# A three-part block on one core: grouped attention turned by block transposes and transfers instead of TensorE, and an end in two halves

## The chip, the cores and the metric

The kernel runs on one core of a Trainium2 chip. The metric is the device time of one execution in microseconds; three executions of the kernel before gave 3020.45, 3019.07 and 3018.32 us, median 3019.07 us. A difference of about 0.2% (6 us) is what such runs can tell from no change.

## The reference

256 tokens of width 2048 pass through two layers and a third, larger block, all in float32. In short:

```python
# layers 0 and 1: u = rms_norm(x) @ w_in; layer 0 pools over 2, 4, 8 and 16 tokens, layer 1 has
# differential attention; both add cross attention to a memory, then x += [..] @ w_out,
# then x += relu(rms_norm(x) @ w_ff1)**2 @ w_ff2
xn = rms_norm_2(x, norm_pre_w); z = xn @ w_in_2            # 2048 -> 13312
u_lru, g_lru, q, k, v, g_attn, m_lru, m_attn = split(z)
h = rg_lru(conv(u_lru), forward) + rg_lru(conv(u_lru), backward)
y_a = h * silu(g_lru)
# 16 query heads in 4 groups over 4 key and value heads of 128, window of +-128 tokens
m = max(scores.max(-1), sink); e = exp(scores - m)
p = e / (e.sum(-1) + exp(sink - m))
y_b = einsum(p, v) * silu(g_attn)
merged = sigmoid(m_lru) * (y_a @ w_proj_a) + sigmoid(m_attn) * (y_b @ w_proj_b)
x = x + rms_norm_2(merged @ w_out_2, norm_post_w)
```

## The kernel before, in words

All matrix products stream weights. A product of 256 tokens with 512 columns of weights is a group; there are 128. A group is eight slabs of 256 weight rows. SyncE loads a slab (512 KB) into one of four buffers `raw`; ScalarE rounds it to `whi` (line 933), VectorE takes the rest `wlo` (line 1260), and TensorE multiplies: 12 products of 128x512 (lines 1790 to 1792), high by high, low by high and high by low, for two row tiles and two token tiles, into `acc0` or `acc1`. A slab's buffer is free once TensorE is through with it, so ScalarE and VectorE can be three slabs ahead.

Everything else hangs between slabs. `plan()` writes, for each engine, which step follows which slab; the engines run their lists in order and meet by semaphores. `attention(j, p)` places one attention job over two heads: `att_in` (TensorE turns queries, and for the grouped jobs keys, by products with the identity, lines 1839 and 1842) after slab p, `att_score` after p+1, `att_smx` and `att_exp` with p+4, `att_prob` with p+5, `att_pt` (eight turns of the probabilities, line 1859) after p+5, `att_pv` (line 1871) after p+6, `att_ot` (four turns of the output, line 1931) after p+7, and `att_o`, `att_hi`, `att_lo` behind. Four jobs are memory attention (two in each layer, placed by `attention` or `roomy`), eight are the grouped attention of the third block. These eight follow one another, one per group of eight slabs. VectorE runs up to three slabs ahead of TensorE, and its step of slab s stands behind its `wlo` of slab s. The softmax scales the output, not the probabilities, by the inverse sum (`att_o`, line 1561), and then by the gate, which GpSimd loads back from DRAM (`gate_load`, line 859).

Where the kernel turns a whole group's output (`turned`), it does so without TensorE: VectorE transposes 32x32 blocks (`turn`, line 1385), and GpSimd moves the blocks to their partitions by 16 transfers of 32 KB (`shuffle`, line 899). One output is still turned on TensorE among the gate groups (`tail`, line 1808). `pool_mix` (lines 1949 to 1951) multiplies each of 12 tiles by the parts of a band matrix that aren't zero.

At the end, `epi_last` squares and scales the last group (lines 1006, 1711), VectorE forms the mean square of both token tiles (`rms`, lines 1271 to 1278), scales and adds in four pieces (line 1766), and SyncE stores four pieces of 512 KB.

## Time and profile before

| | |
|---|---|
| median of three executions | 3019.07 us |
| the profiled execution, its span | 3018.06 us, 3016.3 us |
| PE, DVE, ACT, POOL busy | 2971.2, 1820.8, 1524.8, 442.6 us |
| granted clock over the span | 0.998 |
| share of 16 DMA engines, weight queue and GpSimd's queue | 57.5% and 5.8% |
| a transfer with 256 runs of 512 bytes (`lru_w`) on POOL | 0.72 us |
| a transfer of a shuffle on POOL | 0.50 us |

PE is TensorE, DVE VectorE, ACT ScalarE, POOL GpSimd, SP SyncE. A product is shown with its whole passage through the array (0.39 us for 512 columns), but starts one every 0.23 us, so times of blocks are read from start to start. An f32 product of the attention is recorded as two instructions. "Granted clock" is the share of 2.4 GHz that TensorE was given. An idle time in brackets is that of the engine before the row, with what ended it.

### The profile page before, as it was taken

How to read it: one execution, taken by the hardware profiler on the slowest of the kernel's cores; microseconds unless marked ns; L12 is line 12 of the kernel's file. 1: busy time of each engine (PE TensorE's matmuls, PEld its weight loads, DVE VectorE, ACT ScalarE, POOL GpSimd, SP SyncE). 2: the span in 40 equal slices, each digit the busy share in tenths (PEclk: the TensorE clock that was granted, in tenths of full speed). 3: DMA queues.
4: the chain of work that ended last, by engine and by line, in shares of the span. 5: the costliest groups of instructions: out<-in, count | busy, mean ns of one | idle time of the engine just before them, and what ended most of it. 6: DMA issues, size and time to landing. Idle time of an engine off the chain costs nothing.

```text
span 3016.3 us, 37365 instructions
## 1 busy us (share of the span) xinstructions
PE 2971.2 (99%) x13524; PEld 2461.1 (82%) x13524; DVE 1820.8 (60%) x2399; ACT 1524.8 (51%) x2036; POOL 442.6 (15%) x881
## 2 busy tenths in 40 slices
PE   8999999999999999999999999999999999999998
PEld 7888888888888778778888888888888888787886
DVE  6437555555555776866545555556546668786554
ACT  6535444444444665755434444445445557785443
POOL 0003302011023310012203020122000233010210
PEclk9999999999999999999999999999999999999999
DMA  7556766666567655556666666677666566665774
GB/s 261 168 158 204 217 195 201 204 191 214 180 216 231 205 172 168 152 180 199 216 189 214 192 198 207 188 224 230 199 195 191 175 190 192 192 204 200 248 247 153
DMA packets 326765, 600.08 MB, mean 199 GB/s; under 512 B 31440, under 2 KB 56400, under 8 KB 325840
## 3 DMA queue, kind: packets, MB, share of 16 engines
q1 hardware_dynamic: 293248, 541.13, 57.5%
q0 software_dynamic: 32784, 55.89, 5.8%
q8 instruction: 101, 1.65, 0.2%
q10 hardware_dynamic: 576, 0.94, 0.1%
q14 instruction: 56, 0.46, 0.0%
HBM read 561.15 MB, written 10.49 MB: 190 GB/s over the span
## 4 chain that ended last, share of the span: by engine, by line
PE 89%; DVE 5%; ACT 4%; issue 1%; DMA 0%; DVEq 0%; ACTq 0%; SPq 0%
PE acc L1790 28%; PE acc L1792 28%; PE acc L1791 28%; ACT whi L933 1%; DVE wlo L1255 1%; DVE wlo L1260 1%; PE sd L1871 1%; PE sd L1853 1%; PE tp L1808 1%; ACT prob L1170 1%; PE tp L1960 1%; ACT qk L1178 0%; PE sd L1974 0%; ACT whi L936 0%; PE sd L1859 0%
## 5 line engine op out<-in xcount | busy, mean ns | idle before, releaser
L1790 PE MATMUL acc<-whi,set_hi 128*128 128x512 f32 x4096 | 1616.0, 395 | 16.6 <-DVE wlo L1260 11.0
L1792 PE MATMUL acc<-whi,set_lo 128*128 128x512 f32 x4096 | 1598.2, 390 | 0.0
L1791 PE MATMUL acc<-wlo,set_hi 128*128 128x512 f32 x4096 | 1597.2, 390 | 0.0
L1260 DVE TENSOR_TENSOR wlo<-raw,whi 128x1024 fp32r<-128x1024 f32 x944 | 1136.2, 1221 | 712.9 <-ACT whi L933 711.8
L933 ACT ACTIVATE whi<-raw 128x1024 fp32r<-128x1024 f32 x944 | 980.2, 1057 | 844.8 <-PE acc L1792 672.5
L1790 PEld LDWEIGHTS acc<-whi,set_hi 128*128 128x128 f32 x4096 | 770.5, 188 | 187.2 <-DVE wlo L1260 17.1
L1792 PEld LDWEIGHTS acc<-whi,set_lo 128*128 128x128 f32 x4096 | 769.9, 188 | 161.5
L1791 PEld LDWEIGHTS acc<-wlo,set_hi 128*128 128x128 f32 x4096 | 770.8, 188 | 155.2
L899 POOL DMA_DIRECT2D u<-u x576 | 281.3, 497 | 1516.1 <-DVE u L1385 1328.0
L1255 DVE SCALAR_TENSOR_TENSOR wlo<-raw,par,whi 128x512 fp32r<-128x512 f32 x160 | 111.7, 746 | 49.6 <-ACT whi L936 48.8
L936 ACT ACTIVATE whi<-raw,par 128x512 fp32r<-128x512 f32 x160 | 103.7, 714 | 18.4 <-DMA raw<-in_w_kv 10.3
L1292 DVE TENSOR_TENSOR stage_b<-stage_a 128x1024 f32<-128x1024 f32 x32 | 39.2, 1225 | 103.6 <-ACT stage_a L984 103.6
L984 ACT ACTIVATE stage_a<-acc,small 128x512 f32<-128x512 f32 x64 | 40.5, 686 | 105.2 <-PE acc L1792 105.2
L899 POOL DMA_DIRECT2D kv<-kv x112 | 54.9, 498 | 179.6 <-DVE kv L1385 177.4
L1757 DVE TENSOR_TENSOR x<-acc,x 128x1024 f32<-128x1024 f32 x24 | 29.4, 1224 | 74.9 <-PE acc L1792 74.9
L899 POOL DMA_DIRECT2D x<-x x112 | 55.0, 503 | 32.8 <-DVE x L1385 31.6
L1365 DVE TENSOR_TENSOR set_lo<-u,set_hi 128x1024 fp32r<-128x1024 f32 x36 | 44.0, 1221 | 21.6 <-ACT set_hi L1062 12.3
L1023 ACT ACTIVATE qk<-x 128x512 f32<-128x512 f32 x40 | 25.0, 629 | 39.6 <-DVE x L1287 39.6
L1368 DVE TENSOR_TENSOR set_lo<-tp,set_hi 128x1024 fp32r<-128x1024 f32 x10 | 12.2, 1224 | 47.8 <-ACT set_hi L1069 47.8
L1372 DVE SCALAR_TENSOR_TENSOR set_lo<-tp,par,set_hi 128x256 fp32r<-128x256 f32 x44 | 18.2, 477 | 32.8 <-ACT set_hi L1072 32.8
L1069 ACT ACTIVATE set_hi<-tp 128x1024 fp32r<-128x1024 f32 x10 | 10.3, 1027 | 52.1 <-PE tp L1808 52.1
L1056 ACT ACTIVATE set_hi<-u 128x1024 fp32r<-128x1024 f32 x27 | 28.3, 1050 | 10.3 <-DMA u<-u 10.1
(249 smaller groups left out, 1314.0 us busy)
## 6 DMA issues: line engine op xcount, KB each, us to landing
raw<-in_w_ff SPq DMA_DIRECT2D x512, 512.0 KB, 4.5
raw<-in_w_in SPq DMA_DIRECT2D x248, 512.0 KB, 4.4
raw<-in_w_out SPq DMA_DIRECT2D x96, 512.0 KB, 4.4
u<-u POOLq DMA_DIRECT2D x576, 32.0 KB, 4.6
raw<-in_w_mem_kv SPq DMA_DIRECT2D x32, 512.0 KB, 4.8
raw<-in_w_proj_a SPq DMA_DIRECT2D x32, 512.0 KB, 4.0
raw<-in_w_proj_b SPq DMA_DIRECT2D x32, 512.0 KB, 6.3
raw<-in_w_kv SPq DMA_DIRECT2D x48, 256.0 KB, 3.2
```

The costliest lines, as they stand in the source:

```text
L899: dma(turned[32 * d:32 * (d + 1), 256 * q:256 * (q + 1)], blocks[32 * q:32 * (q + 1), 256 * d:256 * (d + 1)]).then_inc(sm["shuffled"], 16)
L933: A_(whi[:, c], raw[:, c], ACT.Copy).then_inc(w_hi, 1)
L936: ins = A_(whi[:, c], raw[:, c], ACT.Copy, scale=gain_of(fold, SLAB_K * s + t))
L984: ins = A_(stage_a[:, GW * b:GW * (b + 1)], a[:, GW * b:GW * (b + 1)], ACT.Relu, scale=rstd[k][:, b:b + 1])
L1170: ins = A_(prob[:, o:o + TOK], sd[:, (2 * d + k) * TOK:(2 * d + k + 1) * TOK], ACT.Tanh, bias=lruc[:, c:c + 1], scale=0.5)
L1255: ins = V.scalar_tensor_tensor(out=wlo[:, c], in0=raw[:, c], scalar=gain_of(fold, SLAB_K * s + t), in1=whi[:, c].bitcast(f32), op0=ALU.mul ...
L1260: V.tensor_tensor(wlo[:, c], raw[:, c], whi[:, c].bitcast(f32), ALU.subtract).then_inc(w_lo, 1)
L1292: V.tensor_tensor(stage_b[:], stage_a[:], stage_a[:], ALU.mult).then_inc(sm["staged"], 1)
L1365: ins = V.tensor_tensor(in_blocks(l[:, c]), tp, in_blocks(h[:, c]).bitcast(f32), ALU.subtract)
L1790: T.matmul(o, h[:, tok], whi[:, c], start=first, stop=False)
L1791: T.matmul(o, h[:, tok], wlo[:, c], start=False, stop=False)
L1792: ins = T.matmul(o, l[:, tok], whi[:, c], start=False, stop=last)
```

## The change

- Queries and keys of the grouped attention are turned once, right behind their projection (`turn_heads`): VectorE's blocks and 16 transfers for each of four query groups and the keys, with runs of 32 elements. `att_in` is gone from these jobs.
- The grouped jobs are placed by `grouped`: scores after slab p+1, values after p+8. Between them VectorE multiplies the probabilities by the inverse sums (`att_prob`, now in all 12 jobs), transposes their 32x32 blocks in one instruction (`att_turn`), and GpSimd moves them into `qk` by 16 transfers (`att_shuffle`). `att_pt` is gone from these jobs.
- The values are the standing operand, the probabilities stream: two products of 512 columns per grouped job, four of 256 per memory job. The output comes out turned, so `att_ot` is gone from all 12 jobs; `att_o` is one multiplication by the gate, which is turned too (`turn_gate`) and loaded by four transfers.
- The last output that TensorE turned among the gate groups is turned like the others.
- `pool_mix` takes the whole band matrix: two products of 256 columns per tile instead of three of 128, 2 to 16, and 128.
- The last group's last four slabs are taken token tile by token tile, and the end (square, scaling, mean square, sum, store) is done for each half by itself, in five stores.

```diff
...
+    def grouped(self, j, p):
+        for name, off in (("score", 1), ("pv", 8)):
+            self.at("pe", p + off, "att_" + name, j)
+        for name, off in (("exp", 4), ("hi", 12)):
+            self.at("act", p + off, "att_" + name, j)
+        for name, off in (("smx", 4), ("prob", 5), ("turn", 5), ("o", 11), ("lo", 12)):
+            self.at("dve", p + off, "att_" + name, j)
+        self.at("pool", p + 5, "att_shuffle", j)
...
-        for name, off in (("in", 0), ("score", 1), ("pt", 5), ("pv", 6), ("ot", 7)):
+        for name, off in (("in", 0), ("score", 1), ("pt", 5), ("pv", 6)):
...
+        sc.info["queries", i] = sc.heads(S * (g + 1) + 5, ("queries", i), f"q{i}")
...
+    sc.info["keys"] = sc.heads(S * (k + 1) + 5, ("keys", 0), "k")
...
+        sc.at("dve", S * (g + 1) + 4, "turn_gate", i, g)
...
-        sc.attention(B2J + j, S * (ga[1] + j) + 4)
+        sc.grouped(B2J + j, S * (ga[1] + j) + 4)
...
+            def att_shuffle(j):
+                i = j - B2J
+                if i:
+                    pool.wait_ge(sm["prob_in"], 256 * i)
+                    pool.wait_ge(sm["att_pv"], j)
+                pool.wait_ge(sm["prob_tp"], i + 1)
+                blocks = prob_blocks[i // 4]
+                for q in range(4):
+                    for d in range(4):
+                        dma(qk[32 * d:32 * (d + 1), 256 * q:256 * (q + 1)],
+                            blocks[32 * q:32 * (q + 1), 256 * d:256 * (d + 1)]).then_inc(sm["prob_in"], 16)
...
                for q in range(4):
...
+                        to = turned[32 * d:32 * (d + 1), 256 * q:256 * (q + 1)]
+                        of = blocks[32 * q:32 * (q + 1), 256 * d:256 * (d + 1)]
+                        if t is None:
+                            to = in_blocks(turned[32 * d:32 * (d + 1), :])[:, :, q, :]
+                            of = of.rearrange("p (n t) -> p n t", t=32)
+                        dma(to, of).then_inc(sm["shuffled"], 16)
...
             run(S * GALL + 1)
+            for b in range(TB):
+                last_half(act, b)
+                A_(qk[:, GW * b:GW * (b + 1)], acc[(GALL - 1) % 2][:, GW * b:GW * (b + 1)], ACT.Square,
+                   accum_out=fin_ss[:, 4 * b + 3:4 * b + 4]).then_inc(sm["ysq_ok"], 1)
...
+            def turn_heads(n, source, room):
+                if n > sc.info["queries", 0]:
+                    dve.wait_ge(sm["shuffled"], 256 * n)
+                kind, i = source
+                dve.wait_ge(sm["rope"], 5 if kind == "keys" else i + 1)
+                for b in range(TB):
+                    rows = mkv[:, GW * b:GW * (b + 1)] if kind == "keys" else u[:, D * b + GW * i:D * b + GW * (i + 1)]
+                    o = rooms[room][0].rearrange("p (d m b t) -> p b m d t", d=4, m=4, b=TB)[:, b]
+                    ins = V.transpose(o, rows.rearrange("p (m d t) -> p m d t", m=4, d=4))
+                ins.then_inc(sm["heads_tp"], 1)
...
                 _, _, den, rden = stats[0]
                 if j >= B2J:
                     link(V.tensor_tensor(den, den, esink, ALU.add))
-                V.reciprocal(rden, den).then_inc(sm["att_prob"], 1)
+                link(V.reciprocal(rden, den))
+                for r in range(4):
+                    pr = prob[:, TOK * r:TOK * (r + 1)]
+                    ins = V.tensor_scalar(pr, pr, rden[:, r:r + 1], None, ALU.mult)
+                ins.then_inc(sm["att_prob"], 1)
...
             def att_o(j):
                 dve.wait_ge(sm["att_pv"], at(j + 1))
...
+                dve.wait_ge(sm["att_lo"], at(j))
+                dve.wait_ge(sm["ga_in"], 64 * (j - B2J + 1))
+                V.tensor_tensor(in_blocks(ob[:]), in_blocks(sd[:, 0:2 * TOK]),
+                                ga.rearrange("p (q n t) -> p n q t", q=4, t=32), ALU.mult).then_inc(sm["att_o"], 1)
+            def att_turn(j):
+                i = j - B2J
+                dve.wait_ge(sm["att_prob"], j + 1)
+                if i:
+                    dve.wait_ge(sm["prob_in"], 256 * i)
+                if i == 4:
+                    dve.wait_ge(sm["ga_out"], 64)
+                o = prob_blocks[i // 4].rearrange("p (d n t) -> p n d t", d=4, t=32)
+                V.transpose(o, prob[:].rearrange("p (n d t) -> p n d t", d=4, t=32)).then_inc(sm["prob_tp"], 1)
...
+            for b in range(TB):
+                last_half(dve, b)
+                dve.wait_ge(sm["ysq_ok"], 4 + b)
+                c = 3 * GW
+                V.tensor_tensor(y[:, D * b + c:D * b + c + GW], acc[(GALL - 1) % 2][:, GW * b:GW * (b + 1)],
+                                gpost[:, c:c + GW], ALU.mult)
+                link(V.tensor_reduce(fin_rs[:, b:b + 1], fin_ss[:, 4 * b:4 * b + 4], AX.X, ALU.add))
+                link(rms(fin_rs[:, b:b + 1], fin_rs[:, b:b + 1], D, 1))
+                for _, c, n in FINAL[2 * b:2 * b + 2 + b]:
+                    c = slice(D * b + c, D * b + c + n)
+                    V.scalar_tensor_tensor(out=y[:, c], in0=y[:, c], scalar=fin_rs[:, b:b + 1], in1=x[:, c],
+                                           op0=ALU.mult, op1=ALU.add).then_inc(sm["fin_ok"], 1)
...
+            def last_slabs(g, src):
+                for b in range(TB):
+                    for s in range(S - RAW, S):
+                        pe.wait_ge(w_lo, S * g + s + 1)
+                        ins = products(acc[g % 2], src, s, s, b, False, s == S - 1)
+                        if b:
+                            ins.then_inc(mm, 1)
+                    if b == 0:
+                        ins.then_inc(sm["half_out"], 1)
...
                 ins.then_inc(sm["att_pt"], 1)
             def att_pv(j):
-                pe.wait_ge(sm["att_ptc"], at(j + 1))
+                if j < B2J:
+                    pe.wait_ge(sm["att_ptc"], at(j + 1))
+                else:
+                    pe.wait_ge(sm["prob_in"], 256 * (j - B2J + 1))
                 pe.wait_ge(*gout((sc.info["mem"][j // (MH // 2)] if j < B2J else sc.info["k2"]) + 1))
-                for r in range(4):
+                pt = qk[:].rearrange("p (r k q) -> p k r q", r=4, k=2)
+                qt = qk[:].rearrange("p (q r k t) -> p k r q t", q=4, r=4, k=2)
+                if j < B2J:
+                    parts = [(2 * h, 2 * h + 2, MD * (2 * (j % 2) + h)) for h in range(2)]
+                else:
+                    parts = [(0, 4, HD2 * ((j - B2J) // 2))]
+                for of, to, c in parts:
                     for k in range(2):
-                        if j < B2J:
-                            c = 2 * GW + GW * k + MD * (2 * (j % 2) + r // 2)
-                        else:
-                            c = 2 * GW + GW * k + HD2 * ((j - B2J) // 2)
-                        ins = T.matmul(sd[:, P * r:P * (r + 1)], qk[:, (2 * r + k) * P:(2 * r + k + 1) * P],
-                                       mkv[:, c:c + P], start=k == 0, stop=k == 1)
+                        v = mkv[:, 2 * GW + GW * k + c:2 * GW + GW * k + c + P]
+                        p = pt[:, k, of:to] if j < B2J else qt[:, k]
+                        ins = T.matmul(sd[:, P * of:P * to], v, p, start=k == 0, stop=k == 1)
                 ins.then_inc(sm["att_pv"], 1)
...
                     s, n = gout(g - 1)
                     pe.wait_ge(s, n)
                 for t in range(PGT):
-                    old, new = (u[:, D * b + PG * i + P * t:][:, 0:P] for b in range(TB))
-                    o, m = tp[:, TOK * t:TOK * (t + 1)], poolm[:, TB * i * TOK:(TB * i + TB) * TOK]
-                    over = P + WINDOWS[i]
-                    T.matmul(o[:, P:TOK], new, m[:, TOK + P:2 * TOK], start=True, stop=False)
-                    T.matmul(o[:, P:over], old, m[:, P:over], start=False, stop=True)
-                    ins = T.matmul(o[:, 0:P], old, m[:, 0:P], start=True, stop=True)
+                    for b in range(TB):
+                        c = D * b + PG * i + P * t
+                        m = (TB * i + b) * TOK
+                        ins = T.matmul(tp[:, TOK * t:TOK * (t + 1)], u[:, c:c + P], poolm[:, m:m + TOK],
+                                       start=b == 0, stop=b == TB - 1)
```

TensorE's list between two scores of the grouped attention. Before: `att_pt`, `att_pv`, `att_ot` and `att_in` stand there (the rows of slabs, 12 each, are left out).

```order
L1853 MATMUL sd<-qk 128x256 x4
...
L1859 MATMUL sd<-const,prob 128x128 x8
...
L1871 MATMUL sd<-mkv,qk 128x128 x8
...
L1931 MATMUL sd<-const,ob 128x128 x4
...
L1839 MATMUL sd<-const,u 128x128 x4
L1842 MATMUL sd<-const,mkv 128x128 x2
```

Now, in the same place (`x` holds turned queries, `mkv` turned keys, `qk` turned probabilities):

```order
L1965 MATMUL sd<-mkv,x 128x256 x4
L1903 MATMUL acc<-whi,set_hi 128x512
L1904 MATMUL acc<-wlo,set_hi 128x512
...
L1905 MATMUL acc<-whi,set_lo 128x512
L1990 MATMUL sd<-qk,mkv 128x512 x2
```

Seven slabs (84 rows) stand between the scores and the product with the values, where before there were five with a block of turns among them.

VectorE's list behind the scores of a grouped job, before (line 1260 is `wlo` of a slab):

```order
L1495 SCALAR_TENSOR_TENSOR prob<-sd,const 128x512 x2
L1498 TENSOR_REDUCE small<-prob 128x4
L1501 TENSOR_TENSOR small<-small,row 128x4
L1503 TENSOR_TENSOR small<-row,small 128x4
L1505 TENSOR_SCALAR small<-small 128x4
L1260 TENSOR_TENSOR wlo<-raw,whi 128x1024
L1512 TENSOR_TENSOR small<-small 128x4
L1513 RECIPROCAL small<-small 128x4
L1260 TENSOR_TENSOR wlo<-raw,whi 128x1024 x3
L1347 COPY kv<-x 128x256 x2
L1385 STREAM_TRANSPOSE x<-stage_b 128x4x4x32 x2
```

Now, with the four scalings (line 1587) and the block transpose (line 1643) behind the reciprocal:

```order
L1566 SCALAR_TENSOR_TENSOR prob<-sd,const 128x512 x2
L1569 TENSOR_REDUCE small<-prob 128x4
L1572 TENSOR_TENSOR small<-small,row 128x4
L1574 TENSOR_TENSOR small<-row,small 128x4
L1576 TENSOR_SCALAR small<-small 128x4
L1319 TENSOR_TENSOR wlo<-raw,whi 128x1024
L1583 TENSOR_TENSOR small<-small 128x4
L1584 RECIPROCAL small<-small 128x4
L1587 TENSOR_SCALAR prob<-prob,small 128x256 x4
L1643 STREAM_TRANSPOSE u<-prob 128x8x4x32
L1319 TENSOR_TENSOR wlo<-raw,whi 128x1024 x3
L1406 COPY kv<-u 128x256 x2
L1442 STREAM_TRANSPOSE u<-stage_b 128x4x4x32 x2
```

The scalings and the transpose stand before the next slab's `wlo`.

GpSimd's list in two groups of the middle of this stretch, before:

```order
L859 DMA kv<-gate_spill 128x2x256 x2
L899 DMA x<-x 32x256 x16
L859 DMA kv<-gate_spill 128x2x256
L899 DMA x<-x 32x256 x16
L859 DMA kv<-gate_spill 128x2x256
L899 DMA x<-x 32x256 x16
```

Now, with 16 transfers of probabilities (line 904) behind the 16 of a group's output (line 955), and four for the gate:

```order
L904 DMA qk<-kv 32x256 x16
L892 DMA kv<-gate_spill 32x4x128 x4
L955 DMA u<-u 32x256 x16
L904 DMA qk<-u 32x256 x16
L892 DMA kv<-gate_spill 32x4x128 x4
L955 DMA u<-u 32x256 x16
L904 DMA qk<-u 32x256 x16
```

## Rows read from the trace of the kernel before

**Rows 1.** Page, part 1: busy time, share of the span, instructions of each engine.

```profile
PE 2971.2 (99%) x13524; PEld 2461.1 (82%) x13524; DVE 1820.8 (60%) x2399; ACT 1524.8 (51%) x2036; POOL 442.6 (15%) x881
```

**Rows 2.** Timeline of PE: start us, us, engine, line, operation, out<-in, count.

```profile
2389.22 0.60 PE L1839 MATMUL sd<-const,u 128*128 128x128 f32 x4
...
2389.79 0.48 PE L1790 MATMUL acc<-whi,set_hi 128*128 128x512 f32 x1
...
2392.64 1.89 PE L1853 MATMUL sd<-qk 128*128 128x256 f32 x8
...
2394.17 0.58 PE L1790 MATMUL acc<-whi,set_hi 128*128 128x512 f32 x1
...
2397.09 0.39 PE L1790 MATMUL acc<-whi,set_hi 128*128 128x512 f32 x1
...
2405.26 1.04 PE L1859 MATMUL sd<-const,prob 128*128 128x128 f32 x8
...
2406.05 0.48 PE L1790 MATMUL acc<-whi,set_hi 128*128 128x512 f32 x1
...
2408.87 1.95 PE L1871 MATMUL sd<-mkv,qk 128*128 128x128 f32 x16
...
2410.57 0.48 PE L1790 MATMUL acc<-whi,set_hi 128*128 128x512 f32 x1
...
2413.39 0.60 PE L1931 MATMUL sd<-const,ob 128*128 128x128 f32 x4
...
2413.74 0.48 PE L1790 MATMUL acc<-whi,set_hi 128*128 128x512 f32 x1
```

**Rows 3.** Timeline of DVE and ACT behind the scores of that job.

```profile
2399.82 1.99 ACT L933 ACTIVATE whi<-raw 128x1024 fp32r<-128x1024 f32 x2
...
2402.23 0.18 DVE L1513 RECIPROCAL small<-small 128x4 f32<-128x4 f32 x1
```

**Rows 4.** Timeline: scaling on DVE, block transposes on DVE, first transfer on POOL.

```profile
1214.03 0.55 DVE L1545 TENSOR_SCALAR prob<-prob,small 128x128 f32<-128x128 f32 x2
...
2463.43 1.30 DVE L1385 STREAM_TRANSPOSE x<-stage_b 128x512 f32<-128x512 f32 x2
...
2465.32 1.03 POOL L899 DMA_DIRECT2D x<-x  x2 [13.81 <-DVE x L1385]
```

**Rows 5.** Timeline of POOL: one shuffle of 16 transfers.

```profile
2386.26 7.84 POOL L899 DMA_DIRECT2D x<-x  x16
```

**Rows 6.** DMA issues in three short windows: count, KB each, median us to landing.

```profile
x<-x POOLq DMA_DIRECT2D x2, 32.0 KB, 3.8
...
x<-x POOLq DMA_DIRECT2D x5, 32.0 KB, 3.2
...
kv<-kv POOLq DMA_DIRECT2D x2, 32.0 KB, 5.7
```

**Rows 7.** Timeline of PE: two idle times, in brackets, with what ended them.

```profile
1288.17 0.34 PE L1903 MATMUL tp<-qk 64*128 64x128 f32 x1 [2.21 <-ACT stage_b L1130]
...
2747.01 0.51 PE L1790 MATMUL acc<-whi,set_hi 128*128 128x512 f32 x1 [1.80 <-DVE wlo L1260]
```

**Rows 8.** Windows behind these idle times: busy by engine, granted clock, DMA share.

```profile
1289.00:1292.50 3.50, 3.50 (x22) 2.71 (x19) 3.43 (x7) 0.97 (x2) 0.00 (x0) 1.00 0.32 64
...
2747.60:2751.00 3.40, 3.40 (x9) 2.64 (x8) 3.05 (x5) 1.76 (x3) 0.56 (x1) 0.50 0.81 294
```

**Rows 9.** Timeline of PE: one tile of the pooling products, start to start.

```profile
184.17 0.38 PE L1949 MATMUL tp<-kv,u 128*128 128x128 f32 x2
...
184.84 0.39 PE L1949 MATMUL tp<-kv,u 128*128 128x128 f32 x2
```

**Rows 10.** Timeline of the end: last product, squares, final scaling.

```profile
3002.41 0.39 PE L1792 MATMUL acc<-whi,set_lo 128*128 128x512 f32 x1
...
3002.84 0.60 ACT L1006 ACTIVATE qk<-acc 128x512 f32<-128x512 f32 x1 [9.76 <-PE acc L1792]
...
3008.02 4.87 DVE L1766 SCALAR_TENSOR_TENSOR kv<-kv,small,x 128x1024 f32<-128x1024 f32 x4
```

214 lines of the change are left out of this document (113 added, 101 removed).

## Prediction

> **What bounds the kernel now.** I read the busy times first: PE is busy 2971.2 of 3016.3 us, DVE 60%, ACT 51%, POOL 15% [rows 1]. So what PE does is the time, and a step off PE costs nothing until PE waits for it. Then I read PE's timeline over one grouped attention job, always from start to start [rows 2]. Three slabs lie between 2397.09 and 2405.26, so a slab is 2.72 us. Behind a foreign block the next slab is longer: 2.92 us behind the scores (2394.17 to 2397.09), 2.82 us behind the turned probabilities (2406.05 to 2408.87). Nothing in this stretch waits; PE goes from block to block. The third view is the chain on DVE, ACT and POOL that runs from the scores to the values, because the change lengthens it. The last is the end of the trace.
>
> **What PE saves.** Per grouped job, from rows 2: queries and keys 2389.22 to 2389.79 is 0.57, with 0.13 more for the slab behind (2389.79 to 2392.64 is 2.85), 0.70 in all. Probabilities 2405.26 to 2406.05 is 0.79, plus 0.10: 0.89. Output 2413.39 to 2413.74 is 0.35, plus about 0.10: 0.45. Sum 2.04, times 8 jobs 16.3 us. The four memory jobs lose their output turns too: 4 x 0.45 = 1.8. The values' product streams as many columns as before: eight of 128 take 1.70 (2408.87 to 2410.57), four of 256 take 1.53 (the scores, 2392.64 to 2394.17) with a dearer slab behind, so 0.07 saved in each of 12 jobs, 0.8. The last TensorE turn of an output is eight turns, like the probabilities: 0.9. In `pool_mix`, a tile takes 0.67 now [rows 9]; two products of 256 at 1.53/4 are 0.77 to 0.8, so 12 tiles cost 1.2 to 1.8 more, and I take 1.5.
>
> **The end.** Before, the last product starts at 3002.41, two squares follow from 3002.84, and the last scaling starts at 3008.02 and takes 4.87 for four pieces of 1024 [rows 10]. That is 5.61 us from product to scaling, two thirds of it small dependent instructions that stay. Now one half is done while PE still multiplies the other: 24 products, 5.4 us. On the end's path one square goes (0.6), one multiplication by the gain goes (about 0.65, a 512-wide block operation [rows 4]), and of the scaling half goes (2.4), together 3.6. The first half keeps DVE until about 0.4 us after it is wanted, so 3.2 us are saved. PE's own rate doesn't suffer: the first half takes 1.36 us per slab, and the last slab's rest, begun when the first of these four slabs begins, takes about 2.5 us and is wanted after 4.1. Savings in all: 16.3 + 1.8 + 0.8 + 0.9 + 3.2 - 1.5 = 21.5 us.
>
> **The wait that comes in.** In the new list seven slabs stand between a job's scores and its product with the values. From the slab behind the scores (2394.17) that is 2.92 + 6 x 2.72 = 19.2 us [rows 2]. What must fit into it: DVE has the reciprocal of the sums at 2402.41, 8.24 us after that slab's start; in between lie the mask, the maximum, the exponentials (ACT is free at 2399.82), and one slab's `whi` and `wlo`, whose order is unchanged [rows 3]. Then four scalings of 128x256: a pair of 128 and 256 takes 0.55 [rows 4], so four of 256 about 1.15, to 9.4. The block transpose of 128x1024 is the pair of 512-wide ones (1.30) in one, 1.25, and with the semaphores 10.7. POOL starts 0.59 after a transpose has ended (2464.73 to 2465.32 [rows 4]): 11.3. Its 16 transfers take 7.84 [rows 5], the last begins 7.34 after the first: 18.6. It lands 3.8 later [rows 6], and PE starts at 22.5. PE therefore waits 3.3 us for every job. It is in order, so the three slabs that are ready behind the product wait as well, and the next scores too; DVE and ACT stop three slabs ahead. The bounds are the landing: 3.2 us at its shortest, 5.7 at its longest [rows 6], so 2.7 to 5.2 us of wait. I take the value of this stretch, 3.3. Eight jobs: 26.4 us, bounds 21.6 to 41.6.
>
> POOL itself is free in time. It begins a group's gate loads once the output of the job before is multiplied, about 2.9 us after that job's values begin; four of them at about 0.7 and one shuffle of 7.84 end 13.5 us after, and the probabilities come no earlier than 17.
>
> Here the Trainium skill speaks otherwise: "DMA: Bandwidth & Descriptors", section "Anatomy of one DMA — SWDGE (gpsimd) path", gives 2.0 us plus bytes over 436 GB/s, which for 32 KB makes an estimate of 2.1 us for a transfer. No group of rows 6 shows that; they have 3.2 to 5.7. By the page the wait would be 1.6 us per job; what that would give is among the rivals.
>
> **The clock.** A wait costs more than itself where PE's clock falls. Behind an idle time of 1.80 us PE was granted 0.50, the level of 1.2 GHz, for 3.4 us; behind one of 2.21 us it stayed at 2.4 GHz [rows 7, 8]. At half rate 3.4 us of work lose 1.7. A wait of 3.3 us is longer than both, so I expect a fall behind most, some of it spent while PE still waits: 1.2 us per job, 9.6 in all, bounds 0 and 13.6.
>
> **What stays hidden.** DVE gains two transposes per turned group and the scalings, and loses two thirds of `att_o`; at 60% busy, and with nothing of it between a slab's `wlo` and its need, I cost it at nothing. The memory jobs have scalings before their turn of the probabilities, 1.15 us, with more than 3 us of room. The queries' and keys' transfers have runs of 128 bytes, which the trace does not show between SBUF places; bounds are the same time as now (0.50 a transfer, landing as in rows 6), and four times the engines' time per packet. Each set has a whole group of 22 us before the next and more before its first use, so I take nothing, and keep the upper end as a rival.
>
> The same page of the Trainium skill, section "Why small descriptors are slow (HBM only)", says that transfers within SBUF are spared the penalty of short runs; no row shows it, and by it the upper end falls away.
>
> **Sum.** -21.5 + 26.4 + 9.6 = +14.5. The profiled execution took 3018.06 us: 3032.6. The median of the runs is 1 us above it, so I predict 3033 us.
>
> **Rivals.**
> - *The transfers are hidden* (the landing in the gap is faster, or the chain to the reciprocal is). Everything saved stays: 3018.1 - 21.5 = 2996.6. It needs 3.3 us less than rows 3 to 6 add up to, and no row is that short. It decides where the chain is under 19.2 us. Chance 0.10.
> - *Transfers land 1.7 us sooner than the 3.8 of rows 6.* The wait is 1.6 us, shorter than the idle time behind which the clock fell [rows 7]: 8 x 1.6 = 12.8, so -8.7, 3009. Rows 6, with nothing under 3.2, speak against it. Chance 0.06. (This is where the page's figure leads.)
> - *PE waits, but its clock stays up*, as in the first of rows 7: +4.9, 3023. Chance 0.18; this is within 0.2% for the most part.
> - *Long landings*: 5.2 us of wait and a full fall each time, -21.5 + 41.6 + 13.6 = +33.7, 3052. For it: shuffles elsewhere land later. Against: those of this stretch land in 3.2 to 3.8. Chance 0.11.
> - *The short runs clog the DMA engines* beside the weights in the five groups of queries and keys, so that slabs come late: at four times the packet time a shuffle's 512 KB would take a quarter of the engines in a group, which with the 63% of the whole span is near full; some 2 us in each of five groups on top of the forecast, 3043. Chance 0.05.
>
> My forecast has 0.50. Faster by over 0.2% (6 us, about what runs of this kernel can tell from no change): the first two and a little, 0.17. Within 0.2%: most of the third and the low edge of the forecast, 0.16. Slower: 0.67. The likeliest case's own range is 3022 to 3046; the range, down to the second rival and up into long landings, is 3009 to 3050.
>
> **What would show it.** In the changed profile PE's waits should name a DMA into `qk` before the product of 128x512 with `mkv` eight times, 2.7 to 4 us each, and windows behind them should show a clock of 0.50. DVE's transpose should end some 10.7 us after the slab behind the scores starts, and POOL's 16 transfers about 8 us later. The groups without attention should keep 2.72 us a slab, and the store should end 3 us sooner after the last product. If the product starts without a wait, the chain is mis-sized; if the wait is there with the clock at 1.00, only that term is wrong. A wait elsewhere in this stretch, of PE for `wlo`, would mean that DVE or the weight loads are late, which I cost at nothing.

## The result, and the profile after

| | before | after |
|---|---|---|
| median of the runs, us | 3019.76 (3018.32 to 3020.98, 4 runs) | 3051.13 (3050.41 to 3055.41, 4 runs) |
| ratio, 95% interval | | 1.0105 (1.0093 to 1.0117) |
| profiled execution, us | 3018.06 | 3051.75 |
| its span, us; mean granted clock | 3016.3 | 3049.8; 0.992 |

The change makes the kernel 31.4 us slower. The direction was predicted; 3033 was 18 us too low, and 3051 lies just above the range.

Part 1 of the page of the changed kernel answers to [rows 1]:

```profile
PE 2974.9 (98%) x13204; PEld 2442.2 (80%) x13204; DVE 1847.0 (61%) x2469; ACT 1513.6 (50%) x2020; POOL 571.5 (19%) x1129
```

PE has 320 products fewer and yet is busy 3.7 us longer: some of them ran at half clock. POOL's share has grown, as it now turns the probabilities. The list of PE's waits (what it waited for: us in total, times, longest) tells which waits are new:

```profile
PE acc L1903 <- DVE wlo L1319: 16.8, 22, 1.8
PE sd L1990 <- DMA qk<-u: 14.7, 4, 5.2
PE sd L1990 <- DMA qk<-kv: 13.1, 4, 3.6
```

L1990 is `att_pv`, and it waits 8 times, once per grouped job, 27.8 us in all: the wait that the prediction named. The first row has a counterpart before, with seven waits fewer in the whole kernel:

```profile
PE acc L1790 <- DVE wlo L1260: 11.0, 15, 1.8
```

One job, from the timelines of PE, DVE and POOL (start us, us, engine, line, operation, out<-in, count, idle before and what ended it; rows of L1903 to L1905 between them are left out):

```profile
2285.65 1.89 PE L1965 MATMUL sd<-mkv,x 128*128 128x256 f32 x8
2287.19 0.58 PE L1903 MATMUL acc<-whi,set_hi 128*128 128x512 f32 x1
...
2299.05 0.50 PE L1903 MATMUL acc<-whi,set_hi 128*128 128x512 f32 x1 [0.61 <-DVE wlo L1319]
...
2307.12 0.39 PE L1905 MATMUL acc<-whi,set_lo 128*128 128x512 f32 x1
2311.08 3.78 PE L1990 MATMUL sd<-qk,mkv 128*128 128x512 f32 x4 [3.57 <-DMA qk<-kv]
2313.87 1.41 PE L1903 MATMUL acc<-whi,set_hi 128*128 128x512 f32 x1
```

```profile
2295.25 0.18 DVE L1584 RECIPROCAL small<-small 128x4 f32<-128x4 f32 x1
2295.47 1.14 DVE L1587 TENSOR_SCALAR prob<-prob,small 128x256 f32<-128x256 f32 x4
2296.64 1.25 DVE L1643 STREAM_TRANSPOSE kv<-prob 128x1024 f32<-128x1024 f32 x1
2297.81 2.32 DVE L1319 TENSOR_TENSOR wlo<-raw,whi 128x1024 fp32r<-128x1024 f32 x2
```

```profile
2298.49 8.18 POOL L904 DMA_DIRECT2D qk<-kv  x16 [11.91 <-DVE kv L1643]
```

Counted from the slab behind the scores (2287.19), the reciprocal ends at 8.24, the scaling at 9.42, the blocks at 10.70, POOL begins at 11.30 and issues the last transfer at about 19.0. PE starts the product at 23.9. Above it stands a second wait: 0.61 us for `wlo`, whose DVE instruction begins at 2297.81, behind the scaling and the transpose. It comes in all eight jobs (5.0 us in all); in the kernel before, PE waits for nothing in this stretch.

Windows over that job (start:end and length, busy by engine, granted clock, DMA share, GB/s): while POOL issues, while PE waits, and the product:

```profile
2298.50:2306.20 7.70, 7.16 (x31) 5.93 (x32) 7.66 (x10) 3.19 (x3) 7.70 (x16) 1.00 0.78 227
2306.20:2311.00 4.80, 1.30 (x6) 0.75 (x4) 1.70 (x2) 1.06 (x1) 1.01 (x2) 0.88 0.92 283
...
2311.00:2315.00 4.00, 3.92 (x5) 1.83 (x6) 0.11 (x1) 0.00 (x0) 0.00 (x0) 0.50 0.71 278
```

The clock is at 0.50, the level of 1.2 GHz, through the product; that product takes 2.79 us to the next slab (2311.08 to 2313.87) where it takes 1.42 at full clock (below). And the 16 DMA engines are 92% busy just while PE waits. With what? SP's issues in narrow windows:

```profile
2303.33 0.37 SPq L813 DMA_DIRECT2D raw<-in_w_in  x1
...
2305.66 0.37 SPq L813 DMA_DIRECT2D raw<-in_w_in  x1
...
2306.79 0.37 SPq L813 DMA_DIRECT2D raw<-in_w_in  x1
...
2307.93 0.37 SPq L813 DMA_DIRECT2D raw<-in_w_in  x1
```

Four weight loads of 512 KB in 4.6 us. Each `wlo` that DVE makes lets SP issue a load: SP waits for the `wlo` of the slab four before (line 796), so the buffer `raw` comes free there, and not when TensorE is through with the slab, as the description of the kernel has it. DVE makes only one `wlo` between the scores and the blocks; behind them it catches up. The second view is the DMA issues (count, KB each, median us to landing) in two windows, the first and the last of the 16 transfers:

```profile
qk<-kv POOLq DMA_DIRECT2D x2, 32.0 KB, 2.8
...
qk<-kv POOLq DMA_DIRECT2D x2, 32.0 KB, 4.3
```

The very last takes 4.9 (issued at about 2306.2, PE runs at 2311.08). A store of 512 KB to `gate_spill` stands in POOL's queue right behind it, but only in the first three jobs, where the last transfers land in 4.5 to 4.9 us; in the other five they take 3.7 to 5.3.

The end answers to [rows 10]:

```profile
3039.19 0.39 PE L1873 MATMUL acc<-whi,set_lo 128*128 128x512 f32 x1
...
3039.61 0.60 ACT L1295 ACTIVATE qk<-acc 128x512 f32<-128x512 f32 x1 [4.75 <-PE acc L1873]
...
3043.58 2.61 DVE L1855 SCALAR_TENSOR_TENSOR kv<-kv,small,x 128x1024 f32<-128x1024 f32 x3
```

From the last product to the end of the span it is 10.6 us; before, 13.9.

### The profile page after: what moved, and what is told of

Its sections match the earlier page's. It is cut to its first block, busy times and chain, and to the rows that moved or that the text cites. A ratio compares the mean times of both kernels' runs of the same rounds, so it can differ in the third digit from the quotient of the medians.

```text
span 3049.8 us, 37040 instructions
## 1 busy us (share of the span) xinstructions
PE 2974.9 (98%) x13204; PEld 2442.2 (80%) x13204; DVE 1847.0 (61%) x2469; ACT 1513.6 (50%) x2020; POOL 571.5 (19%) x1129
## 4 chain that ended last, share of the span: by engine, by line
PE 81%; DVE 8%; ACT 6%; issue 2%; POOL 2%; DMA 2%; ACTq 0%; DVEq 0%; POOLq 0%
PE acc L1903 25%; PE acc L1905 25%; PE acc L1904 25%; POOL qk L904 2%; ACT whi L988 2%; DVE wlo L1319 1%; PE sd L1990 1%; DVE wlo L1314 1%; PE sd L1965 1%; DMA qk<-u 1%; DMA qk<-kv 1%; ACT prob L1225 1%; PE tp L1921 1%; PE tp L2071 1%; ACT qk L1233 0%
## 5 line engine op out<-in xcount | busy, mean ns | idle before, releaser
L1903 PE MATMUL acc<-whi,set_hi 128*128 128x512 f32 x4080 | 1615.2, 396 | 23.0 <-DVE wlo L1319 16.8
L1905 PE MATMUL acc<-whi,set_lo 128*128 128x512 f32 x4080 | 1592.8, 390 | 0.0
L1903 PEld LDWEIGHTS acc<-whi,set_hi 128*128 128x128 f32 x4080 | 769.1, 189 | 202.3 <-DVE wlo L1319 26.2
L1905 PEld LDWEIGHTS acc<-whi,set_lo 128*128 128x128 f32 x4080 | 768.1, 188 | 161.7
L955 POOL DMA_DIRECT2D u<-u x704 | 344.1, 497 | 1551.1 <-DVE u L1442 1361.6
L1990 PE MATMUL sd<-qk,mkv 128*128 128x256 f32 (+1 forms) x64 | 33.9, 675 | 27.8 <-DMA qk<-u 14.7
L955 POOL DMA_DIRECT2D x<-kv x64 | 36.8, 583 | 63.4 <-DVE kv L1454 45.0
L1990 PEld LDWEIGHTS sd<-qk,mkv 128*128 128x128 f32 x64 | 14.0, 232 | 38.9 <-DMA qk<-u 16.4
L1442 DVE STREAM_TRANSPOSE u<-stage_b 128x512 f32<-128x512 f32 x64 | 41.7, 690 | 0.8
L904 POOL DMA_DIRECT2D qk<-kv x64 | 32.3, 513 | 49.9 <-DVE kv L1643 49.9
```

Of the source, the lines that this page charges most:

```text
L904: dma(qk[32 * d:32 * (d + 1), 256 * q:256 * (q + 1)], blocks[32 * q:32 * (q + 1), 256 * d:256 * (d + 1)]).then_inc(sm["prob_in"], 16)
L955: dma(to, of).then_inc(sm["shuffled"], 16)
L1442: ins = V.transpose(o, source_rows(source, b).rearrange("p (m d t) -> p m d t", m=4, d=4))
L1903: T.matmul(o, h[:, tok], whi[:, c], start=first, stop=False)
L1905: ins = T.matmul(o, l[:, tok], whi[:, c], start=False, stop=last)
L1990: ins = T.matmul(sd[:, P * of:P * to], v, p, start=k == 0, stop=k == 1)
```

## Experiments

Theory: all of the loss is PE's wait at the values' product and the clock that falls behind it, and the wait is long because the weight loads share the DMA engines with the turned probabilities. Rivals: the landing is these transfers' own; or the loss is spread over the stretch by the added DVE work and transfers. Each kernel is the changed one with the edit shown. The results:

| run | us, median (range) | ratio to before, 95% |
|---|---|---|
| `e_fill` wait filled with products | 3038.05 (3036.6 to 3039.7) | 1.0059 (1.0042 to 1.0076) |
| `e_nowait` product waits for nothing | 3006.43 (3005.8 to 3008.3) | 0.9958 (0.9941 to 0.9974) |
| `e_tiny` weight loads cut | 3013.79 (3012.6 to 3015.6) | 0.9981 (0.9971 to 0.9991) |
| `e_split` issue shared with ACT | 3017.19 (3014.0 to 3019.1) | 0.9988 (0.9979 to 0.9998) |
| `e_late` product one slab later | 3024.05 (3022.7 to 3026.4) | 1.0015 (1.0005 to 1.0024) |
| `e_split_late` | 3014.41 (3012.6 to 3016.3) | 0.9984 (0.9974 to 0.9993) |
| `e_slm` and old pool_mix | 3013.25 (3011.7 to 3016.2) | 0.9979 (0.9969 to 0.9989) |
| `e_oldend` old end | 3054.45 (3053.5 to 3055.9) | 1.0116 (1.0099 to 1.0133) |
| `e_hold` load of slab 11 held | 3033.69 (3032.6 to 3034.8) | 1.0047 (1.0030 to 1.0064) |
| `e_split_hold` | 3015.90 (3014.5 to 3018.6) | 0.9987 (0.9977 to 0.9996) |
| `e_shm` and old pool_mix | 3014.96 (3013.5 to 3018.1) | 0.9985 (0.9976 to 0.9995) |
| `e_shm6` and blocks later | 3012.10 (3010.4 to 3014.9) | 0.9975 (0.9965 to 0.9985) |
| `e_hold12` load of slab 12 held | 3015.48 (3014.3 to 3018.9) | 0.9987 (0.9978 to 0.9996) |
| `e_best` split, slab 12 held, old pool_mix, blocks later | 3006.55 (3005.0 to 3009.4) | 0.9960 (0.9946 to 0.9973) |
| `e_sm6` `e_best` without the held load | 3017.27 (3013.6 to 3019.3) | 0.9993 (0.9984 to 1.0002) |

### The wait filled

```
                 else:
+                    for _ in range(12):
+                        T.matmul(tp[:, 0:GW], h0[:, 0:P], h0[:, GW:2 * GW], start=True, stop=True)
                     pe.wait_ge(sm["prob_in"], 256 * (j - B2J + 1))
```

> The changed kernel with 12 products of 128x512 put ahead of the wait for the turned probabilities in each of the 8 grouped jobs; their result is not used. They stand inside the 2.7 to 5.4 us for which TensorE waits there, so the wait itself keeps its end. Theory (an idle of 3 us and more drops the granted clock, and the stretch at half clock costs some 2 us a job): the clock stays at 1.00 through the values' products in most jobs, the 34.1 us at half clock in the attention stretch go to under 10, and the time falls by 12 to 16 us, to 3035 to 3039 us. Rival (the values' products of 512 columns are slow behind any wait, whatever the clock): 3050 to 3052 us, with the values' products at the same length as now.

Measured 3038.05, 13.1 us less than the changed kernel, with 96 products more. PE's timeline of the same job, and the window over it; then the whole attention stretch of this kernel and of the changed one:

```profile
2307.71 2.88 PE L1980 MATMUL tp<-set_hi 128*128 128x512 f32 x12
2310.59 1.98 PE L1993 MATMUL sd<-qk,mkv 128*128 128x512 f32 x4
2312.01 0.79 PE L1903 MATMUL acc<-whi,set_hi 128*128 128x512 f32 x1
```

```profile
2308.00:2312.00 4.00, 4.00 (x16) 2.51 (x15) 0.26 (x1) 1.06 (x1) 0.00 (x0) 1.00 0.96 317
...
2256.00:2500.00 244.00, 232.51 (x973) 181.92 (x972) 149.82 (x224) 99.47 (x169) 123.12 (x245) 0.99 0.61 185
```

```profile
2256.00:2506.00 250.00, 217.22 (x856) 165.31 (x855) 146.73 (x220) 97.75 (x167) 118.16 (x235) 0.94 0.57 176
```

The clock is at 1.00 and the product takes 1.42 us (2310.59 to 2312.01). So 13 us of the loss (12.0 in the traces, over the attention stretch) are clock and nothing else; the rival, products slow by themselves, falls. One job still fell (a wait of 2.7 us was left there).

### The product that waits for nothing

```
-                    pe.wait_ge(sm["prob_in"], 256 * (j - B2J + 1))
+                    pe.wait_ge(sm["shuffled"], 256 * (sc.info["keys"] + 1))
...
-                        p = pt[:, k, of:to] if j < B2J else qt[:, k]
+                        p = pt[:, k, of:to] if j < B2J else rooms[f"q{(j - B2J) // 2}"][1][:, GW * k:GW * (k + 1)]
```

> The changed kernel with the 8 value products of grouped attention reading the room of the turned queries in place of the turned probabilities, so that they wait for nothing of their own job: the real attention product is left out, all transfers and VectorE's blocks are still there. It measures what the change saves where its chain of waits costs nothing. Theory (everything lost is the wait and the clock behind it): 3051 less 29.1 of waits less some 16 of clock, plus nothing: 3003 to 3008 us if the waits on wlo stay, 2997 to 3001 us if they go too. Rival (part of the loss is the contention of 256-descriptor transfers and VectorE's blocks with the rest of the pipeline): above 3012 us with no single wait to name.

Measured 3006.43: 13.8 us below before, although every transfer, scaling and block is still done. The rival of a loss spread over the stretch falls. The changed kernel's 44.7 us above this one are the wait and what hangs on it. The waits for `wlo` stay here, and so does the long landing: the median of three late transfers of one job is 4.0 us (below), and over the jobs the last one lands 23.0 to 25.6 us behind the slab next to the scores, as in the changed kernel. So it isn't PE's wait that makes the landing long.

```profile
qk<-kv POOLq DMA_DIRECT2D x3, 32.0 KB, 4.0
```

### The weight loads cut

```
+                elif g.reg is None and 98 <= g.base <= 106:
+                    sp.dma_start(dst.rearrange("p (t n) -> p t n", t=SLAB_K)[:, :, 0:16],
+                                 src[:, 0:16].rearrange("(t p) n -> p t n", p=P)).then_inc(ld[s % RAW], 16)
```

> The changed kernel with the weight loads of groups 98 to 106 cut from 512 to 16 columns (the rest of these weights is left out), so that the transfers of the turned probabilities have the 16 DMA engines nearly to themselves. Theory (the weight loads that catch up while the 16 transfers are issued share the DMA engines with them, and that makes the landing 4.5 to 5.3 us): the landing behind the last issue falls to 1.7 to 2.5 us, TensorE's wait by 2 to 3 us a job, the time by 16 to 30 us with the clock, to 3021 to 3035 us. Rival (the landing is the transfers' own): still 4 to 5 us, and 3048 to 3052 us.

Measured 3013.79, further down than the theory's range, as nearly all of the clock's loss went too. The DMA issues over that job:

```profile
qk<-kv POOLq DMA_DIRECT2D x16, 32.0 KB, 1.7
```

POOL issues at the same pace (2295.29, 8.20 us for 16), but the median landing is 1.7 us, where the changed kernel has 3.6 (and 4.9 for the last), and PE waits 3.5 us in all where it waited 27.8. The landing is not the transfers' own. What this kernel can't tell is whether that gain is to be had with all weights loaded; the held load below does.

The Trainium skill, "DMA: Bandwidth & Descriptors", section "Anatomy of one DMA — SWDGE (gpsimd) path", makes an estimate of 2.1 us for 32 KB; the 1.7 us of this row are near it, and the prediction was right that the busy engines' rows don't show it. The section "Queues, rings and completion order" has each DMA engine take turns between the queues that have work for it, a packet at a time; the 4.9 us beside four loads are what such sharing would give, but no run here shows the turns themselves.

### The issue shared out, and the product later

ACT issues half of the transfers from its list at slab 8 (`prob_ia` counts them):

```
+        self.at("act", p + 8, "att_shuffle", j)
...
-                for q in range(4):
+                for q in range(2):
...
+            def att_shuffle(j):
+                ...
+                for q in (2, 3):
+                    for d in range(4):
+                        act.dma_start(qk[32 * d:32 * (d + 1), 256 * q:256 * (q + 1)], ...).then_inc(sm["prob_ia"], 16)
```

> The changed kernel with the 16 transfers of each turned probability tile shared out: GpSimd issues 8, ScalarE's queue the other 8 from its list three slabs later. Theory (the issue of 16 transfers, 7.4 us on one engine, is the longest piece of the chain and halves): last issue at 14.9 instead of 18.6 us behind the scores, landed at 18 to 20 against a slot at 19.2, TensorE's wait 0 to 1 us a job, clock up: 3003 to 3012 us. Rival (the DMA engines, not the issue, set the landing): landed at 22 to 23 as now, 3045 to 3052 us. A second rival: the 8 issues delay ScalarE's casts of the weights, and TensorE waits on whi: 3015 to 3030 us.

Measured 3017.19: neither of the first two. The time lies in the second rival's range, but PE nowhere waits for `whi`, so that is not its cause. ACT's and POOL's issues, and the landing of the last ones:

```profile
2293.27 5.01 ACTq L1170 DMA_DIRECT2D qk<-kv  x8
...
2293.76 4.29 POOL L906 DMA_DIRECT2D qk<-kv  x8 [11.92 <-DVE kv L1660]
```

```profile
qk<-kv POOLq DMA_DIRECT2D x3, 32.0 KB, 4.9
...
qk<-kv ACTq DMA_DIRECT2D x2, 32.0 KB, 5.4
```

In the mean of the eight jobs the last issue is 3.8 us sooner (15.2 for 19.0), but the last landing only 2.4 (21.4 for 23.8): the transfers now come twice as densely beside the same loads, and the last one takes 5.0 to 7.7 us. 9 us of waits are left, in one job with a fall of the clock.

`e_late` changes one number, `("pv", 8)` to `("pv", 9)`.

> The changed kernel with the values' products of the 8 grouped jobs one slab later (9 slabs behind the job's start instead of 8), nothing else. Theory (it is the distance in TensorE's queue that is too short): the products' slot moves from some 20.2 to 22.6 us behind the slab next to the scores; what lands at 23.0 to 23.9 then leaves 0.4 to 1.4 us of wait (3 us in job 4), which is too short to cost the clock. The next scores, two slabs later, wait up to 1 us for the gated output. Waits fall from 29 to some 8 to 14 us, the clock keeps 1.00: 3014 to 3026 us. Rival (the transfers land with the weight loads, so that TensorE running sooner through its slabs brings the loads and the landing later too): 3035 to 3050 us.

Measured 3024.05, inside. PE's waits in the stretch:

```profile
PE sd L1965 <- issue: 5.8, 7, 0.8
PE acc L1903 <- DVE wlo L1319: 4.8, 8, 0.6
PE sd L1990 <- DMA qk<-u: 4.2, 3, 2.6
PE sd L1990 <- DMA qk<-kv: 2.5, 3, 1.3
```

6.7 us at the product instead of 27.8, clock up; but the next scores (L1965) follow directly behind the product now, not two slabs behind as the expectation had it, and wait 0.8 us each for the gated output (the profile names no releaser, but `att_score` waits for `att_o` of the job before). With both edits, and then with the old pool_mix:

> The changed kernel with both: 8 of the 16 transfers issued by ScalarE's queue, and the values' products one slab later. With the transfers shared out alone TensorE still waited 0.2 to 2.9 us a job (10.5 us in all), and the turned tile had landed 20.1 to 22.4 us behind the slab next to the scores. Theory (only the chain against the slot counts): a slot at 22.6 us lies behind all these landings, so no wait on them is left; with what the job without any wait took (3006.4 us) as the floor, 3006 to 3011 us, the rest being the wait of the next scores for the gated output. Rival (ScalarE's part of the issue delays its casts of the weights, or the next scores wait over 1 us for the output): 3014 to 3020 us.

> The same with the banded products of pool_mix as they were before the change. Theory: pool_mix cost 1.16, 0.9 and 0.8 us at its groups, so 3 us less than the kernel with both: 3003 to 3008 us, 0.4 to 0.55% faster than before. Rival (what the start of those groups lost comes from another part of the change there, the loads or the clock): the same time as the kernel with both.

Measured 3014.41 and 3013.25. No wait on the transfers is left, but 5.8 us at the scores and 4.9 us on `wlo` are, so the first is 3 us above its range and on the rival's side, and the second 5 us above its own. In `e_slm` the step of 1.16 us at group 7 is gone; the difference of the medians, 1.2 us, is a third of what was expected and within what these runs can tell. The traces say more: over groups 4 to 7, where all of `pool_mix` stands, `e_slm` gains 2.4 us on `e_split_late`, and it loses 1.7 again at 1286 us, where its clock falls and that of `e_split_late` doesn't. The changed kernel's other step, 0.9 us up to the start of group 27, is not at a `pool_mix`.

### The end alone

Edit: the last four slabs, the sums, the scaling and the stores as before the change.

> The changed kernel with the end as it was before: the last slabs over both halves of the tokens, one pass of the sums, four stores of equal size. Theory (the end in halves gives 3.2 us, 13.85 to 10.63 us from the last product to the end, and nothing else): 3054.0 to 3055.0 us, and the way from the last product to the end back at 13.8 us. Rival (part of what the halves gave was taken back ahead of the last product, as its slabs wait for all four slabs' weights): 3051.5 to 3053 us.

Measured 3054.45, 3.3 us above the changed kernel, as expected. The last product and the last scaling of this kernel:

```profile
3038.38 0.39 PE L1896 MATMUL acc<-whi,set_lo 128*128 128x512 f32 x1
...
3043.99 4.87 DVE L1846 SCALAR_TENSOR_TENSOR kv<-kv,small,x 128x1024 f32<-128x1024 f32 x4
```

### One load held

```
+                        j = g - (sc.info["k2"] + 3) - 1
+                        if 0 <= j < H2 // 2 and s == S - 1:
+                            sp.wait_ge(sm["prob_in"], 256 * (j + 1))
                         slab(N(g), s, W[of.w], N(of.row), N(of.col), k, of.pieces)
```

> The changed kernel with one wait more: SyncE holds the weight load of one slab per grouped job (the one 11 behind the job's start, with whose low part VectorE begins after the gated output) until that job's turned probabilities have landed; the loads behind it stand in the same queue and wait too. All work is done. In the changed kernel these four loads are issued 16.0 to 20.6 us behind the slab next to the scores, and their low parts are made at 28 us and later. Theory (the loads share the DMA engines with the 16 transfers and make their landing 4.5 us instead of 1.7 to 2.1 as with the loads cut): landed at 20.5 to 21.5 us, waits of TensorE under 1 us a job beside job 4, clock up, 3012 to 3020 us. Rival (the two loads issued at 11.7 and 12.9 us, which stay, are enough to slow the transfers): landed at 22.5 us and later, 3030 to 3050 us. Second rival: the held loads come late to the next slabs, and TensorE waits on whi or wlo there: 3020 us and more, with these waits in the list.

Measured 3033.69: the landing as by the theory, the time not. POOL's issues, the landing of the last three, and PE at the next scores:

```profile
2297.78 8.21 POOL L907 DMA_DIRECT2D qk<-kv  x16 [11.82 <-DVE kv L1646]
```

```profile
qk<-kv POOLq DMA_DIRECT2D x3, 32.0 KB, 1.7
```

```profile
2314.43 2.47 PE L1968 MATMUL sd<-mkv,x 128*128 128x256 f32 x5 [2.45 <-issue]
```

Full-size weights, 1.7 us. But I had held one load too early: DVE makes the low part of slab 11 ahead of `att_o`, so the gated output and the next scores were late (`att_o` ends at 2314.33, the scores start at 2314.43), 15.1 us in seven jobs, with the clock falling behind four of them. `e_hold12` holds the next slab's (`- 2` for `- 1`, `s == 0` for `s == S - 1`):

> The changed kernel with the held weight load one slab further (12 behind the job's start). In the run with the load of slab 11 held, the tile landed 1.7 us behind its last issue in each job, but VectorE makes the low part of slab 11 ahead of the gated output, and that output, and TensorE's next scores behind it, came 2.1 us late in the median. The low part of slab 12 stands behind the output. Theory (only the held load being one too early cost the 15.1 us of waits at the scores): the landing is 1.7 to 2.5 us again, the waits at the scores go, a wait of 0.1 to 0.7 us a job at the values' products stays (2 us in job 4), with the clock at 1.00: 3011 to 3018 us. Rival (holding any load for 7 to 9 us makes the next slabs late): 3022 to 3035 us with waits on wlo or at the scores.

Measured 3015.48, inside the range and 35.6 us below the changed kernel by one wait of SP. PE's waits in the stretch:

```profile
PE acc L1906 <- DVE wlo L1322: 5.8, 8, 0.8
PE sd L1993 <- DMA qk<-u: 3.1, 4, 1.9
PE sd L1993 <- DMA qk<-kv: 2.2, 4, 0.8
```

The scores wait no longer, the product 5.3 us in all, and the clock never falls in the stretch. The last transfers land in 1.7 to 2.4 us in all eight jobs. This is the run that settles it: contention with the weight loads, with all work done, accounts for 22.5 of the 27.8 us of wait, and for all falls of the clock in the stretch.

### The held load with the rest, and the best version

These three have the load of slab 11 held (the mistake was not known yet); `e_shm6` also moves `("turn", 5)` to `("turn", 6)`.

> The kernel with the 16 transfers shared out between GpSimd and ScalarE, and the same held loads. Shared out alone the tiles landed at 20.1 to 22.4 us, 5.5 to 7.6 us after the last issue at 14.6 to 15.1, against a slot of TensorE at some 20.2 us. Theory: with the loads held they land at 17 to 19.5 us, no wait on them is left, and the time is that of the kernel whose products wait for nothing (3006.4 us): 3005 to 3009 us. Rival (16 transfers on two queues at once are bound by the DMA engines or their descriptors, with or without loads): landed after 20.2 us, 3011 to 3017 us.

> The same with the banded products of pool_mix as before the change. Theory: these are 4 jobs with 0.3 us more product time and one in front of a wait; group 7 alone lost 1.16 us by them: 3003.5 to 3007.5 us, some 1.2 to 1.5 us under the kernel without this edit. Rival: no difference that can be told (under 0.5 us).

> The same, and the blocks of probabilities one slab later in VectorE's list, behind the low part for which TensorE waited 0.6 us a job. Theory: the wait on wlo goes (some 0.8 us a job with what it costs around it, 6 us in all), the chain to the turned tile is 1.2 us longer and still ends before the products' slot, which is 0.8 us sooner: 2997 to 3002 us. Rival (the slot and the landing meet again): waits on the transfers of 0.3 to 1 us a job in their place, 3002 to 3008 us.

Measured 3015.90, 3014.96 and 3012.10. The tiles land at 17.4 to 18.9 us as expected and PE waits for no transfer, but the scores wait 7.7, 8.7 and 11.7 us, the mistake's price; so none of the three reached its range. In the third the wait on `wlo` is gone from the stretch, and with nothing waited for the product starts 19.24 us behind the slab after the scores, where it started at 20.15 in `e_nowait` and `e_split_hold`: the `wlo` wait costs 0.9 us a job.

> All together: the 16 transfers shared out, the weight load of slab 12 held, pool_mix as before the change, the blocks of probabilities one slab later in VectorE's list. Theory: no wait on the transfers, none on wlo, none at the scores: the kernel without any wait took 3006.4 us, pool_mix gives back 1.2 us and the wait on wlo 6 us: 2998 to 3002 us, 0.6 to 0.7% faster than before. Rival (the waits at the scores, 11.7 us with slab 11 held, stay in part because VectorE is full there): 3003 to 3010 us.

> The same without a held load. Theory (the weight loads make the landing 5.5 to 7.6 us with two queues): the tile lands at 21 to 23.5 us against a slot at 19.3 us, waits of 2 to 4 us a job with the clock falling: 3015 to 3035 us. Rival (the chain is so short with two queues that the held load is worth little): 3000 to 3008 us.

`e_best` measured 3006.55, 0.40% faster than before (0.27 to 0.54%), the best of the kernels that do all the work. It missed its range by 4.5 us, since one wait came back; the rival's waits at the scores are not there, though the time is in its range. All of PE's waits in the stretch:

```profile
PE sd L2012 <- DMA qk<-kv: 3.4, 4, 1.0
PE sd L2012 <- DMA qk<-u: 3.1, 4, 1.0
```

With the blocks later and the loads of slabs 10 and 11 in flight beside the transfers again, the product starts at 19.9 to 20.4 us against a slot at 19.24. Without the held load (`e_sm6`, 3017.27, inside its range) the waits are 14.5 us, in one job with a fall of the clock: in that order of work it is worth 10.7 us.

## Why the prediction was off

**What PE saves.** Right in sum. The prediction had 21.5 us, the end and pool_mix included. `e_nowait` is 13.8 us under before and still pays the wait on `wlo`, 8 x 0.9 = 7.3, so the savings are 21.1; in the profiled executions, whose spans are 12.4 us apart, they are 19.7. Of these the attention stretch (from the start of group 97 to that of group 107) has 16.8, for which the forecast had 16.9. For `pool_mix` the forecast had a cost of 1.5 us: over its groups, 4 to 7, the changed kernel falls 1.3 us behind the kernel before, and the old products take 2.4 back (`e_slm`). The end's 3.2 us was measured twice, 10.6 for 13.9 us in the traces and 3.3 by `e_oldend`.

**The chain.** Right up to the issue: 8.24, 9.4, 10.7, 11.3 as forecast, and a last issue at 18.5 to 19.1 for 18.6 (20.4 in one job), 19.0 in the mean.

**The landing.** Wrong, and the size of one term. The prediction took 3.8 us, "the value of this stretch". The mean of the eight jobs is 4.8. The row is from the shuffle that begins at 2386.26 [rows 5], ahead of the job's scores. SP's issues beside it, and behind the scores, in the trace of before:

```profile
2386.12 7.37 SPq L781 DMA_DIRECT2D raw<-in_w_in  x3
...
2402.15 7.81 SPq L781 DMA_DIRECT2D raw<-in_w_in  x5
```

Three loads in 7.4 us, then none for 8.7 us (the softmax holds DVE), then five in 7.8. The shuffle's last transfers landed in the quiet, with one load under way; the turned probabilities are issued into the burst, and the change moves the burst, behind its first load, 2.5 us further towards them by its own work on DVE. These rows stood in the trace of before; I took the nearest shuffle and did not look at which loads it had beside it. PE starts the product at 23.8 us instead of 22.5 in the mean: 1.0 of the 1.3 us is the landing, the rest the last issue.

**"Nothing of it between a slab's `wlo` and its need."** Wrong. The scaling and the blocks, 2.5 us, stand in DVE's queue ahead of a low part for which PE then waits 0.6 us, 0.9 with the slab behind. The text had named this wait as what would contradict it. By itself it moves only the slot, from 19.2 to 20.15; in the changed kernel it hides in the larger wait.

**The clock.** The mechanism was right, the size not. The forecast had 9.6 us. The attention stretch takes 298.7 us in the changed kernel and 254.8 in `e_nowait`, 43.9 more. The distance from the slot (20.15) to the product (23.8) is 8 x 3.64 = 29.1 of them, and 0.9 is the product's own start behind a wait (1.42 for 1.31 us). The rest, about 14 us, is clock; `e_fill`, in which one fall is left, shows 12.0 of it directly. Seven of eight jobs fell, three of them for 6.8 us and four for 3.4, where I had allowed one stretch of 3.4, partly in the wait.

**The sum.** Forecast -21.5 + 26.4 + 9.6 = +14.5. Measured in the profiled executions, in the same terms: -19.7 saved, +36.4 of wait (29.1, and 7.3 from the slot of the forecast, 19.2, to 20.15), +14.8 for the clock and the start, and +2.0 outside the stretch, nearly all of it a fall of the clock at 1289 us that is no effect of the change (below): +33.5, the difference of the spans. By the medians the change costs 31.4 us. So the step that failed is the wait, by 10 us, some 8 of them the landing of 4.8 for 3.8 us and the rest the last issue, and with it the clock behind the wait, by 5. The wait on `wlo`, costed at nothing, adds nothing in this kernel, since PE waits for the later landing anyhow.

**Rivals.** "Long landings" (3052) has the nearest time, and its clock term (13.6) came true; but its landing of 5.7 never came (5.3 at most), and its wait of 41.6 us was 36.4. "The clock stays up" is what `e_fill` made by hand. The short runs of the queries and keys clogged nothing: their 80 transfers cost POOL 583 ns each to issue and land in 2.2 to 4.2 us, and PE waits nowhere for them.

## What to carry over

A landing time belongs to the traffic beside it: before taking one from another place of the trace, list the bulk loads issued there and at the place where the new transfer will stand (an engine that has been held back catches up, and its buffers come free in a burst). Where a short transfer decides, holding the bulk load behind it, one that nobody needs yet, can be worth more than splitting the short one; read on the consumer's queue which load is the first not needed. In this kernel eight waits of 3.5 us in the mean cost about 14 us of clock on top, so each counted as 5.2.

## What the hardware showed that I had not expected

The same idle time need not have the same effect. PE waits 2.21 us for ACT's `stage_b` in all kernels. Before, the clock stayed at 1.00 [rows 7, 8]; in the changed kernel it fell. The wait, and the window behind it (mean clock 0.54); then the same window in `e_oldend`, whose program is the same up to there and where the same wait ends at 1289.25:

```profile
1288.81 0.34 PE L2021 MATMUL tp<-qk 64*128 64x128 f32 x1 [2.21 <-ACT stage_b L1181]
```

```profile
1289.00:1292.50 3.50, 3.50 (x19) 2.63 (x18) 2.34 (x4) 1.56 (x2) 0.00 (x0) 0.54 0.13 32
```

```profile
1289.00:1292.50 3.50, 3.25 (x24) 2.65 (x25) 2.38 (x4) 2.00 (x3) 0.00 (x0) 1.00 0.10 30
```

So the fall at 1289 us differs between executions of the same instructions, and is worth 1.6 us; two profiled executions can differ by that much with no edit as the cause. In the changed kernel's first job 2.7 us of wait brought no fall, in its last one 2.5 us did. In its trace and in that of `e_oldend` every wait of 3.1 us or more at the values' product, thirteen in all, had a fall behind it. What decides below that stays open.

ACT's queue is paced at 0.63 us an issue here (5.01 us for 8), POOL's at 0.5 (8.18 for 16).
